# Splitting the finished mixed rows of two output projections during the attention units ahead of them

## The chip, the cores and the metric

One core of one Trainium2 chip runs the whole program as a single launch. The metric is device time in microseconds, the median of several runs. The engines are TensorE (PE, matmuls; PEld is its loading of stationary weights), VectorE (DVE), ScalarE (ACT), GpSimd (POOL) and SyncE (SP), which here issues nearly all DMAs. Each works through its own queue in order and waits on semaphores.

## The reference

Four residual layers over 256 tokens of width 2048, batch 1, in float32. The first two matter here:

```python
def even_layer(h, w_in, ..., w_out):
    lru_x, lru_gate, q, k, v, swa_gate = split_cols(h @ w_in, EVEN_SPLITS)
    y_a = rg_lru(conv(lru_x), ...) * silu(lru_gate)                # 1024 columns
    y_b = sliding_window_gqa_sinks(q, k, v, sinks) * silu(swa_gate) # 1024 columns
    return jnp.concatenate([y_a, y_b], axis=-1) @ w_out            # 2048 x 2048

def odd_layer(h, w_in, ..., w_out):
    y_c = causal_mla_attention(q, k_c, v_c) * silu(mla_gate)       # 1024 columns
    y_d = rmsnorm(causal_diff_attention(qd, kd, vd, lam), subln) * silu(diff_gate)
    return jnp.concatenate([y_c, y_d], axis=-1) @ w_out            # 2048 x 2048

x = x + even_layer(rmsnorm(x, g0), ...)
x = x + odd_layer(rmsnorm(x, g1), ...)
```

A second block of two layers (retention and Fourier mixing, then a gated convolution) follows, with a context of 256 tokens and shifts, scales and gates that come from conditioning matrices `ada_w`.

## The kernel before

**Precision.** Each float32 operand is split in two: a high half rounded to TensorE's float32r type, and a low half, the difference. A product is three matmuls: high by high, high by low, low by high (L1742 to L1744 where weights are stationary, L1753 to L1755 where activations are). ScalarE writes the high half of weights (`w_hi`, L656), VectorE the low half (`w_lo`, L1159). The projected activations live as both halves in `act` (`act_hl`, 16 tiles of 128 features by 2 x 256 tokens), the split operand of the next projection.

**Stages, units, pieces.** The work is a row of stages: lru, kv, swa, out0, cq, diff, mla, out1, ret, four, out2, conv, out3. A stage is cut in units (an eighth or a quarter of its output columns), a unit in pieces of weights (swa, out0, mla and out1 have 4 units of 8 pieces). A piece is about 128 x 1024 numbers in one of 4 slots: SP loads it to `w_raw`, ScalarE and VectorE split it, TensorE multiplies. A slot is split again when TensorE has used the piece four back (`s_used`, "piece_used"), and loaded again when VectorE has split it (`s_lo`).

**Hooks.** All five engines run the same loop over pieces. After its own step for piece p, an engine calls a hook, `hook(p)`. In unit i + 1 the hook does the rest of unit i: for swa, the hooks compute scores (TensorE, hook 0, L1991), maxima (VectorE, hook 3, L1317 to L1329), exponentials (ScalarE, hook 4), normalised probabilities (VectorE, hook 4, up to L1343), transposes (TensorE, hook 4, L1998), values times probabilities (TensorE, hook 6, L2004 to L2006), and the gated result into `y` (`y_mix`, VectorE, hook 7, L1362). mla is alike, with rotated queries (L1420 to L1423) ahead of the scores and its result at L1432. The hooks of the last unit of swa run in unit 0 of out0, those of mla's last in unit 0 of out1. TensorE issues the last unit's scores before piece 0 of the output projection, and its transposes behind piece 2.

**Mixed rows.** The inputs of an output projection are the 16 tiles of `y`, split into `act` by `mix(stage, q)` in four groups of four tiles: ScalarE copies the high half (L662, from L717), VectorE subtracts (L1262). Group 0 is needed by piece 0 (`inputs_ready`), the next ones by pieces 2, 4 and 6. The order of the groups is

```python
        FOURS = [(4 * q, 4) for q in range(4)]
        GROUPS = {"out0": FOURS, "out1": [FOURS[0], FOURS[2], FOURS[3], FOURS[1]]}
```

so in out0 groups 0 and 1 are the lru rows, in out1 group 0 is the first half of mla, groups 1 and 2 are diff. The last group is the one that the last unit finishes. `act` is the operand of swa's own projections, and of the first four pieces of each mla unit; the other four read `cn` (`c_norm`), the normalised latents, 10 tiles that cq writes. In the kernel before, groups 0 to 2 are split in hook 2 of unit 0 of the output projection, when all pieces of the stage ahead are used.

**Beside it.** VectorE also multiplies and sums conditioning weights (`ada_step`, L1148) in hooks of swa, out0, cq, diff, mla and out1: behind pieces 0, 1, 5 and 6 in swa, behind every piece in mla and in units 1 to 3 of out0. The output projection of unit i is added to `x_res` in hook 2 of unit i + 1 (L1505).

Of the kernel before, what the change touches and what calls it, by code (L numbers as in the profile page):

```python
# [55 lines left out]
COUNT = {s: n for s, n, _ in STAGES}  # L56
# [93 lines left out]
def build(nc, d, out, stop_after=None):  # L150

    ctx = ExitStack()
    with ctx:
# [134 lines left out]
        S = {}  # L288
# [306 lines left out]
        def mix_dst(stage, kt):  # L595
            second = stage in ("out2", "out3") and not (isinstance(kt, int) and kt >= KT)
            return (act2, kt) if second else (act, kt % KT)
# [48 lines left out]
        def _(sc):  # L646
# [400 lines left out]
            if wanted("kv"):  # L1047
                split("kv")(0, lambda p: lru(p, COUNT["lru"] - 1))
                stage_loop(sc, "swa", split("swa"), swa, kv)
            if wanted("out0"):  # L1050
                n = COUNT["swa"] - 1
                post0, sums0 = out_sums("out0")
                stage_loop(sc, "out0", split("out0"), post0, placed({
                    2: [step(swa, 2, n), projections_through("out0"), *mixes("out0", 0, 1, 2), step(swa, 4, n)],
                    5: [step(swa, 6, n)],
                    6: [y_ready("swa"), *mixes("out0", 3)]}))
# [5 lines left out]
            if wanted("diff"):  # L1062
                stage_loop(sc, "diff", split("diff"), diff, cq_end)
                stage_loop(sc, "mla", split("mla"), mla, squeezed(diff, COUNT["diff"] - 1))
            if wanted("out1"):
                n = COUNT["mla"] - 1
                post1, sums1 = out_sums("out1")
                stage_loop(sc, "out1", split("out1"), post1, placed({
                    2: [step(mla, 2, n), projections_through("out1"), *mixes("out1", 0, 1, 2), step(mla, 4, n)],
                    5: [step(mla, 6, n)],  # L1070
                    6: [y_ready("mla"), *mixes("out1", 3)]}))
# [47 lines left out]
        def _(ve):  # L1119
# [546 lines left out]
            if wanted("kv"):  # L1666
                split("kv")(0, lambda p: lru(p, COUNT["lru"] - 1))
                stage_loop(ve, "swa", split("swa"), swa, kv)
            if wanted("out0"):
# [3 lines left out]
                    2: [*mixes("out0", 0), step(swa, 3, n), *mixes("out0", 1, 2), step(swa, 4, n)],  # L1673
# [5 lines left out]
            if wanted("diff"):  # L1679
# [6 lines left out]
                stage_loop(ve, "mla", split("mla"), mla, diff_end)  # L1686
            if wanted("out1"):
# [3 lines left out]
                    2: [step(mla, 3, n), *mixes("out1", 0, 1, 2), step(mla, 4, n)],  # L1691
# [567 lines left out]
```

How the kernel before makes its waits and increments, by code:

```python
            def load_ada(stage, i, a, k):  # L459
                if not isinstance(a, int) or a >= ADA_RING:
                    sp.wait_ge(s_au, a - (ADA_RING - 1))
                layer = 1 if stage in ("ret", "conv") else 0
                first = {"ret": i * ADA_N, "four": (i - 1) * ADA_N + 2 * D, "conv": (i - 1) * ADA_N + 2 * D}
                first = first[stage] if stage in first else a // ADA_K * ADA_N
                w = d["ada_w_2"].rearrange("l (t p) n -> p l t n", p=P)
                sp.dma_start(ada_ring_of(stage)[:, k % ADA_RING, :], w[:, layer, k, ds(first, ADA_N)])\
                    .then_inc(s_aw[k % ADA_RING], 16)
# [2 lines left out]
                def load(i, hook, first=0):  # L471
                    for p in range(PIECES[stage]):
                        g = PIECE0[stage] + PIECES[stage] * i + p
                        pieces = sources(stage, i, p)
                        if not isinstance(g, int) or g >= RING:
                            sp.wait_ge(s_lo, g - (RING - 1))
                        for dst, src in pieces:
                            sp.dma_start(dst(w_raw[:, p % RING, :]), src).then_inc(s_w[p % RING], 16)
                        for a, k in ada_steps(stage, first, i, p):
                            if stage == "ret" and first == 0 and k == 0:
                                sp.wait_ge(s_n["psum"], NORM_BANKS[3] + 8)
                            if stage == "four" and first == 1 and k == 0:
                                sp.wait_ge(S["ret"]["o"], COUNT["ret"])
```

## Time and profile before

| what | value |
|---|---|
| median of 3 runs | 2867.1 us (2862.36 to 2867.46) |
| the profiled execution | 2870.17 us, of which the span 2868.5 |
| TensorE busy | 2737.6 us (95% of the span), loads 2568.2 |
| VectorE busy | 1763.1 us (61%) |
| ScalarE busy | 1280.6 us (45%) |
| DMA | 534.50 MB, 186 GB/s on average |
| mean granted clock of TensorE | 0.978 |

The span runs from the first to the last instruction; the rest of the execution lies around it. Busy shares are averages over all stages. The granted clock is a share of TensorE's 2.4 GHz: 1.00, or 0.50 for 1.2 GHz.

### The profile page before, as it was taken

Reading aid. Unit: us, or ns where it says so; the run is one execution under the profiler, and the core shown is the slowest. Engines: PE = TensorE matmul, PEld = TensorE weight load, DVE = VectorE, ACT = ScalarE, POOL = GpSimd, SP = SyncE. Lnnn points to the kernel's source line nnn. Section 1 sums busy time; section 2 is a strip of 40 time slices with the busy share of each in tenths; the row PEclk is TensorE's granted clock in tenths of the full one; section 3 lists DMA queues with packets and bytes.
Section 4 is the critical chain, followed back from the end, with each engine's and each line's share of the span. In section 5 each row is a group of like instructions: output and inputs, shape, how many; then the busy total and the mean of one; then the engine's idle time right before and its main releaser. Section 6 shows DMA issues by size and latency. Waiting matters only on the chain.

```text
span 2868.5 us, 49783 instructions
## 1 busy us (share of the span) xinstructions
PE 2737.6 (95%) x19249; PEld 2568.2 (90%) x19249; DVE 1763.1 (61%) x2244; ACT 1280.6 (45%) x1670; POOL 18.4 (1%) x33
## 2 busy tenths in 40 slices
PE   7999999998889799999999999999999999999997
PEld 7998789998777699999999987879999999999786
DVE  6777878777656755555556535456675454555544
ACT  5556444554443434443343334444444444444443
POOL 1000000000000000000000000000000000000000
PEclk9999999998889899999999999999999999999999
DMA  6565866655537365555548644547685555555554
GB/s 185 151 196 159 271 185 204 186 178 173 162 129 271 104 197 167 176 177 185 174 156 277 207 147 154 188 144 250 228 292 180 186 182 181 181 180 185 175 189 139
DMA packets 450700, 534.50 MB, mean 186 GB/s; under 512 B 32955, under 2 KB 343750, under 8 KB 449670
## 3 DMA queue, kind: packets, MB, share of 16 engines
q1 hardware_dynamic: 447840, 522.29, 57.5%
q0 software_dynamic: 2064, 10.11, 1.1%
q8 instruction: 92, 1.51, 0.2%
q14 instruction: 42, 0.34, 0.0%
q10 hardware_dynamic: 662, 0.25, 0.0%
HBM read 530.46 MB, written 2.10 MB: 186 GB/s over the span
## 4 chain that ended last, share of the span: by engine, by line
PE 82%; DVE 7%; ACT 3%; DVEq 3%; DMA 2%; issue 2%; ACTq 0%; SPq 0%
PE banks L1742 16%; PE banks L1744 16%; PE banks L1743 16%; PE banks L1753 8%; PE banks L1754 8%; PE banks L1755 8%; DVE w_lo L1159 3%; ACT w_hi L656 2%; PE banks L1991 1%; PE banks L2120 1%; PE banks L2137 1%; PE banks L1899 1%; DVEq L1150 1%; DMA w_raw<-in_od_w_in 1%; DMA w_raw<-in_l_w_in 1%
## 5 line engine op out<-in xcount | busy, mean ns | idle before, releaser
L1159 DVE TENSOR_TENSOR w_lo<-w_raw,w_hi 128x1024 fp32r<-128x1024 f32 (+2 forms) x848 | 974.5, 1160 | 834.1 <-ACT w_hi L656 814.0
L656 ACT ACTIVATE w_hi<-w_raw 128x1024 fp32r<-128x1024 f32 (+2 forms) x848 | 844.4, 1005 | 1088.5 <-PE banks L1744 606.1
L1742 PE MATMUL banks<-act_hl,w_hi 128*128 128x256 f32 x4304 | 1249.1, 290 | 36.0 <-DVE w_lo L1159 17.1
L1744 PE MATMUL banks<-act_hl,w_lo 128*128 128x256 f32 x4304 | 1226.0, 285 | 0.0
L1743 PE MATMUL banks<-act_hl,w_hi 128*128 128x256 f32 x4304 | 1225.9, 285 | 0.0
L1742 PEld LDWEIGHTS banks<-act_hl,w_hi 128*128 128x128 f32 x4304 | 832.9, 194 | 52.3 <-DVE w_lo L1159 18.7
L1743 PEld LDWEIGHTS banks<-act_hl,w_hi 128*128 128x128 f32 x4304 | 832.9, 194 | 3.8 <-issue 2.4
L1744 PEld LDWEIGHTS banks<-act_hl,w_lo 128*128 128x128 f32 x4304 | 832.5, 193 | 0.0
L1753 PE MATMUL banks<-w_hi,act_hl 128*128 128x512 f32 (+3 forms) x1440 | 509.5, 354 | 26.4 <-DVE x_res L1505 7.5
L1754 PE MATMUL banks<-w_lo,act_hl 128*128 128x512 f32 (+3 forms) x1440 | 506.9, 352 | 0.0
L1755 PE MATMUL banks<-w_hi,act_hl 128*128 128x512 f32 (+3 forms) x1440 | 506.2, 352 | 0.0
L1753 PEld LDWEIGHTS banks<-w_hi,act_hl 128*128 128x128 f32 x1440 | 273.8, 190 | 66.4 <-DVE w_lo L1159 13.5
L1755 PEld LDWEIGHTS banks<-w_hi,act_hl 128*128 128x128 f32 x1440 | 273.3, 190 | 32.6
L1754 PEld LDWEIGHTS banks<-w_lo,act_hl 128*128 128x128 f32 x1440 | 273.6, 190 | 31.4 <-issue 0.2
L662 ACT ACTIVATE scr_b<-banks 128x512 f32<-128x512 f32 (+3 forms) x130 | 77.5, 619 | 112.6 <-PE banks L2137 29.8
L1148 DVE SCALAR_TENSOR_TENSOR acc_x<-const_b,silu_c,acc_x 128x512 f32<-128x512 f32 x120 | 89.8, 748 | 4.5
L1148 DVE SCALAR_TENSOR_TENSOR acc_x<-y_mix,silu_c,acc_x 128x512 f32<-128x512 f32 x120 | 89.5, 746 | 1.7
L1148 DVE SCALAR_TENSOR_TENSOR acc_c<-ada_ring,silu_c,acc_c 128x512 f32<-128x512 f32 x120 | 89.4, 745 | 0.1
L1148 DVE SCALAR_TENSOR_TENSOR acc_x<-ada_ring,silu_c,acc_x 128x512 f32<-128x512 f32 x120 | 89.4, 745 | 0.0
L662 ACT ACTIVATE scr_a<-banks 128x512 f32<-128x512 f32 (+2 forms) x68 | 42.4, 662 | 92.4 <-PE banks L1998 55.4
L777 ACT ACTIVATE scr_a<-scr_a,soft 128x128 f32<-128x128 f32 x80 | 35.3, 442 | 52.7 <-DVE soft L1329 52.7
L1932 PE MATMUL banks<-ident,x_res 128*128 128x128 f32 x128 | 21.2, 332 | 20.6 <-DMA x_res<-in_x 10.8
(270 smaller groups left out, 1586.5 us busy)
## 6 DMA issues: line engine op xcount, KB each, us to landing
w_raw<-in_od_w_in SPq DMA_DIRECT2D x256, 512.0 KB, 4.5
w_raw<-in_ev_w_in SPq DMA_DIRECT2D x256, 256.0 KB, 3.6
w_raw<-in_l_w_in SPq DMA_DIRECT2D x96, 512.0 KB, 4.3
w_raw<-in_l_w_in SPq DMA_DIRECT2D x128, 256.0 KB, 3.2
ada_ring<-in_ada_w SPq DMA_DIRECT2D x128, 256.0 KB, 4.3
w_raw<-in_l_w_out SPq DMA_DIRECT2D x64, 512.0 KB, 4.9
y_mix<-in_ada_w SPq DMA_DIRECT2D x128, 256.0 KB, 3.1
const_b<-in_ada_w SPq DMA_DIRECT2D x128, 256.0 KB, 4.5
```

The source lines that it names most:

```text
L656: last = nc.scalar.activation(dst(w_hi[:, p % RING, :]), src(w_raw[:, p % RING, :]), ACT.Copy)
L662: return nc.scalar.activation(dst, src, ACT.Copy, **k)
L777: last = nc.scalar.activation(v[:, h, lo:hi], v[:, h, lo:hi], ACT.Exp, bias=soft[:, 1, 2 * h + b:2 * h + b + 1], accum_out=soft[:, 2, 2 * ...
L1148: last = stt(acc, w, cond, acc, ALU.mult, ALU.add)
L1150: drain()
L1159: last = tt(dst(w_lo[:, p % RING, :]), src(w_raw[:, p % RING, :]), dst(w_hi[:, p % RING, :]).bitcast(F32), ALU.subtract)
L1742: mm(out, hi, a[:, kt, 0:T], start=start, stop=False, skip_group_check=True)
L1743: mm(out, hi, a[:, kt, T:2 * T], start=False, stop=False, skip_group_check=True)
L1744: return mm(out, lo, a[:, kt, 0:T], start=False, stop=stop, skip_group_check=True)
L1753: mm(out, ah, hi, start=start, stop=False, skip_group_check=True)
L1754: mm(out, ah, lo, start=False, stop=False, skip_group_check=True)
L1755: return mm(out, al, hi, start=False, stop=stop, skip_group_check=True)
```

## The change

The whole splits of groups 0 and 1 move ahead. For out0 they go to unit 2 of swa (hooks 0 and 5 on ScalarE, 1 and 6 on VectorE) and write `cn`, which is not in use before cq; TensorE reads these eight tiles there. For out1 they go to unit 3 of mla (hooks 6 and 7 on both engines), when the unit's first four pieces have been used, and write `act` as before; group 2 goes to hook 0 of out1's unit 0. Group 3 stays. TensorE's order of instructions does not change, only an address.

```diff
         def mix_dst(stage, kt):
+            if stage == "out0" and kt < 8:
+                return cn, kt
             second = stage in ("out2", "out3") and not (isinstance(kt, int) and kt >= KT)
...
@@ ScalarE
-                stage_loop(sc, "swa", split("swa"), swa, kv)
+
+                def swa_and_mix(p, i):
+                    swa(p, i)
+                    if i == 1 and p in (0, 5):
+                        sc.wait_ge(S["lru"]["y"], COUNT["lru"] + 1)
+                        mix("out0", p // 5)
+                stage_loop(sc, "swa", split("swa"), swa_and_mix, kv)
...
-                    2: [step(swa, 2, n), projections_through("out0"), *mixes("out0", 0, 1, 2), step(swa, 4, n)],
+                    2: [step(swa, 2, n), projections_through("out0"), *mixes("out0", 2), step(swa, 4, n)],
...
-                stage_loop(sc, "mla", split("mla"), mla, squeezed(diff, COUNT["diff"] - 1))
+                def mla_and_mix(p, i):
+                    mla(p, i)
+                    if i == COUNT["mla"] - 2 and p in (6, 7):
+                        sc.wait_ge(s_used, pieces_before("mla", i + 1) + 4)
+                        mix("out1", p - 6)
+                stage_loop(sc, "mla", split("mla"), mla_and_mix, squeezed(diff, COUNT["diff"] - 1))
...
-                    2: [step(mla, 2, n), projections_through("out1"), *mixes("out1", 0, 1, 2), step(mla, 4, n)],
+                    0: mixes("out1", 2),
+                    2: [step(mla, 2, n), step(mla, 4, n)],
...
@@ VectorE
-                stage_loop(ve, "swa", split("swa"), swa, kv)
+                def swa_and_mix(p, i):
+                    swa(p, i)
+                    if i == 1 and p in (1, 6):
+                        mix("out0", p // 6)
+                stage_loop(ve, "swa", split("swa"), swa_and_mix, kv)
...
-                    2: [*mixes("out0", 0), step(swa, 3, n), *mixes("out0", 1, 2), step(swa, 4, n)],
+                    2: [step(swa, 3, n), *mixes("out0", 2), step(swa, 4, n)],
...
-                stage_loop(ve, "mla", split("mla"), mla, diff_end)
+                def mla_and_mix(p, i):
+                    if i == COUNT["mla"] - 2 and p in (6, 7):
+                        mix("out1", p - 6)
+                    mla(p, i)
+                stage_loop(ve, "mla", split("mla"), mla_and_mix, diff_end)
...
-                    2: [step(mla, 3, n), *mixes("out1", 0, 1, 2), step(mla, 4, n)],
+                    0: mixes("out1", 2),
+                    2: [step(mla, 3, n), step(mla, 4, n)],
```

How instructions move is shown on VectorE, at three places. The numbers of lines are 16 higher in the changed kernel, so L1159, L1262 and L1317 are L1175, L1278 and L1333 there.

In swa's unit 2, before, from the result of unit 0 (`y_mix`) to the start of unit 1's maxima (`soft` are the row statistics, `acc_c` and `acc_x` the conditioning sums):

```order
L1362 TENSOR_TENSOR y_mix<-banks,scr_a 128x512 [waits swa_gate,swa_o]
L1159 TENSOR_TENSOR w_lo<-w_raw,w_hi 128x1024 [waits piece_hi]
L1148 SCALAR_TENSOR_TENSOR acc_c<-ada_ring,silu_c,acc_c 128x512 [waits ada_landed0]
L1148 SCALAR_TENSOR_TENSOR acc_x<-ada_ring,silu_c,acc_x 128x512
L1159 TENSOR_TENSOR w_lo<-w_raw,w_hi 128x1024 [waits piece_hi]
L1148 SCALAR_TENSOR_TENSOR acc_c<-ada_ring,silu_c,acc_c 128x512 [waits ada_landed1]
L1148 SCALAR_TENSOR_TENSOR acc_x<-ada_ring,silu_c,acc_x 128x512
L1159 TENSOR_TENSOR w_lo<-w_raw,w_hi 128x1024 [waits piece_hi] x2
L1317 TENSOR_TENSOR scr_a<-banks,const_a 128x768 [waits swa_scores]
```

and in the changed kernel:

```order
L1378 TENSOR_TENSOR y_mix<-banks,scr_a 128x512 [waits swa_gate,swa_o]
L1175 TENSOR_TENSOR w_lo<-w_raw,w_hi 128x1024 [waits piece_hi]
L1164 SCALAR_TENSOR_TENSOR acc_c<-ada_ring,silu_c,acc_c 128x512 [waits ada_landed0]
L1164 SCALAR_TENSOR_TENSOR acc_x<-ada_ring,silu_c,acc_x 128x512
L1175 TENSOR_TENSOR w_lo<-w_raw,w_hi 128x1024 [waits piece_hi]
L1278 TENSOR_TENSOR c_norm<-y_mix,c_norm 128x4x256 [waits mix_hi]
L1164 SCALAR_TENSOR_TENSOR acc_c<-ada_ring,silu_c,acc_c 128x512 [waits ada_landed1]
L1164 SCALAR_TENSOR_TENSOR acc_x<-ada_ring,silu_c,acc_x 128x512
L1175 TENSOR_TENSOR w_lo<-w_raw,w_hi 128x1024 [waits piece_hi] x2
L1333 TENSOR_TENSOR scr_a<-banks,const_a 128x768 [waits swa_scores]
```

The subtraction of group 0 (`c_norm`) stands behind the `w_lo` of piece 1, ahead of that piece's conditioning sums; that of group 1 stands likewise behind piece 6, further down.

At out0's start, before, from the `w_lo` of the first three pieces, through the maxima of the last swa unit:

```order
L1159 TENSOR_TENSOR w_lo<-w_raw,w_hi 128x1024 [waits piece_hi] x3
L1262 TENSOR_TENSOR act_hl<-y_mix,act_hl 128x4x256 [waits mix_hi]
L1317 TENSOR_TENSOR scr_a<-banks,const_a 128x768 [waits swa_scores]
L1322 TENSOR_REDUCE soft<-scr_a 128x2
L1323 TENSOR_REDUCE soft<-scr_a 128x2
L1326 TENSOR_TENSOR soft<-soft,sinks 128x4
...
L1329 TENSOR_SCALAR soft<-soft 128x4
L1262 TENSOR_TENSOR act_hl<-y_mix,act_hl 128x4x256 [waits mix_hi] x2
L1355 TENSOR_TENSOR soft<-soft 128x4 [waits swa_exp]
```

and in the changed kernel:

```order
L1175 TENSOR_TENSOR w_lo<-w_raw,w_hi 128x1024 [waits piece_hi] x3
L1333 TENSOR_TENSOR scr_a<-banks,const_a 128x768 [waits swa_scores]
L1338 TENSOR_REDUCE soft<-scr_a 128x2
L1339 TENSOR_REDUCE soft<-scr_a 128x2
L1342 TENSOR_TENSOR soft<-soft,sinks 128x4
...
L1345 TENSOR_SCALAR soft<-soft 128x4
L1278 TENSOR_TENSOR act_hl<-y_mix,act_hl 128x4x256 [waits mix_hi]
L1371 TENSOR_TENSOR soft<-soft 128x4 [waits swa_exp]
```

The subtraction of group 0 ahead of the first maxima is gone, and of the two behind the second maxima one is left, that of group 2.

At out1's start, before, from the `w_lo` of the first three pieces (L1420 to L1423 are the rotated queries, then come the maxima of the last mla unit):

```order
L1159 TENSOR_TENSOR w_lo<-w_raw,w_hi 128x1024 [waits piece_hi] x3
L1420 TENSOR_TENSOR scr_a<-banks,const_a 128x256 [waits mla_rot]
L1421 TENSOR_TENSOR scr_a<-scr_a,const_a 128x256
L1423 TENSOR_TENSOR scr_a<-scr_a 128x256
L1317 TENSOR_TENSOR scr_a<-banks,const_a 128x768 [waits mla_scores]
L1322 TENSOR_REDUCE soft<-scr_a 128x2
L1323 TENSOR_REDUCE soft<-scr_a 128x2
L1329 TENSOR_SCALAR soft<-soft 128x4
L1262 TENSOR_TENSOR act_hl<-y_mix,act_hl 128x4x256 [waits mix_hi] x3
L1337 RECIPROCAL soft<-soft 128x4 [waits mla_exp]
```

and in the changed kernel:

```order
L1175 TENSOR_TENSOR w_lo<-w_raw,w_hi 128x1024 [waits piece_hi]
L1278 TENSOR_TENSOR act_hl<-y_mix,act_hl 128x4x256 [waits mix_hi]
L1175 TENSOR_TENSOR w_lo<-w_raw,w_hi 128x1024 [waits piece_hi] x2
L1436 TENSOR_TENSOR scr_a<-banks,const_a 128x256 [waits mla_rot]
L1437 TENSOR_TENSOR scr_a<-scr_a,const_a 128x256
L1439 TENSOR_TENSOR scr_a<-scr_a 128x256
L1333 TENSOR_TENSOR scr_a<-banks,const_a 128x768 [waits mla_scores]
L1338 TENSOR_REDUCE soft<-scr_a 128x2
L1339 TENSOR_REDUCE soft<-scr_a 128x2
L1345 TENSOR_SCALAR soft<-soft 128x4
L1353 RECIPROCAL soft<-soft 128x4 [waits mla_exp]
L1358 TENSOR_TENSOR scr_a<-scr_a,soft 128x2x128
```

The subtraction of group 2 stands between the first `w_lo` and the other two, ahead of the rotated queries; the three behind the maxima are gone.

## Rows read from the trace of the kernel before

**Rows 1.** The page: its span, and the chain that ended last (shares of the span).

```profile
span 2868.5 us, 49783 instructions
...
PE 82%; DVE 7%; ACT 3%; DVEq 3%; DMA 2%; issue 2%; ACTq 0%; SPq 0%
```

**Rows 2.** TensorE's timeline at out0's start: start us, duration us, then line and operation.

```profile
267.66 1.68 PE L1991 MATMUL banks<-scr_a 64*128 64x128 f32 x16
272.61 0.79 PE L1753 MATMUL banks<-w_hi,act_hl 128*128 128x512 f32 x1 [3.27 <-DVE act_hl L1262]
...
275.67 0.39 PE L1754 MATMUL banks<-w_lo,act_hl 128*128 128x512 f32 x1
...
282.02 0.39 PE L1755 MATMUL banks<-w_hi,act_hl 128*128 128x512 f32 x1
```

**Rows 3.** VectorE's timeline, same stretch.

```profile
265.31 3.49 DVE L1159 TENSOR_TENSOR w_lo<-w_raw,w_hi 128x1024 fp32r<-128x1024 f32 x3
...
272.48 0.95 DVE L1317 TENSOR_TENSOR scr_a<-banks,const_a 128x768 f32<-128x768 f32 x1
...
277.47 2.35 DVE L1262 TENSOR_TENSOR act_hl<-y_mix,act_hl 128x1024 fp32r<-128x1024 f32 x2
...
281.99 0.68 DVE L1343 TENSOR_TENSOR scr_a<-scr_a,soft 128x512 f32<-128x512 f32 x1
```

**Rows 4.** ScalarE's timeline, same stretch.

```profile
270.26 2.93 ACT L662 ACTIVATE act_hl<-y_mix 128x1024 fp32r<-128x1024 f32 x3
273.21 1.28 ACT L772 ACT_TABLE_LOAD   x1
...
277.59 0.20 ACT L772 ACTIVATE soft<-soft 128x4 f32<-128x4 f32 x1 [0.53 <-DVE soft L1329]
...
279.46 2.94 ACT L656 ACTIVATE w_hi<-w_raw 128x1024 fp32r<-128x1024 f32 x3
```

**Rows 5.** Windows: us, busy of PE, PEld, DVE, ACT, POOL, then granted clock, DMA.

```profile
240.00:244.00 4.00, 4.00 (x38) 3.58 (x36) 3.91 (x5) 3.92 (x5) 0.00 (x0) 1.00 0.77 243
272.00:276.00 4.00, 3.39 (x9) 2.73 (x10) 3.70 (x9) 3.38 (x8) 0.00 (x0) 0.57 0.17 65
738.00:742.00 4.00, 4.00 (x31) 4.00 (x29) 3.76 (x8) 3.20 (x10) 0.00 (x0) 0.78 0.18 48
816.00:820.00 4.00, 4.00 (x28) 4.00 (x28) 3.84 (x8) 3.52 (x9) 0.00 (x0) 0.72 0.34 96
```

**Rows 6.** TensorE's timeline at out1's start.

```profile
840.90 0.46 PE L1991 MATMUL banks<-scr_a 128*128 128x128 f32 x2 [2.04 <-DVE scr_a L1423]
...
846.19 1.22 PE L1991 MATMUL banks<-k_rope,scr_a 64*128 64x256 f32 x2
850.92 0.80 PE L1753 MATMUL banks<-w_hi,act_hl 128*128 128x512 f32 x1 [3.51 <-DVE act_hl L1262]
...
855.78 0.42 PE L1755 MATMUL banks<-w_hi,act_hl 128*128 128x512 f32 x1
```

**Rows 7.** VectorE's timeline, same stretch.

```profile
836.10 3.50 DVE L1159 TENSOR_TENSOR w_lo<-w_raw,w_hi 128x1024 fp32r<-128x1024 f32 x3
...
849.64 3.49 DVE L1262 TENSOR_TENSOR act_hl<-y_mix,act_hl 128x1024 fp32r<-128x1024 f32 x3
```

**Rows 8.** Timeline of swa unit 2, VectorE and TensorE.

```profile
225.51 0.68 DVE L1343 TENSOR_TENSOR scr_a<-scr_a,soft 128x512 f32<-128x512 f32 x1
...
227.65 1.47 PE L1998 MATMUL banks<-ident,scr_a 128*128 128x128 f32 x12
...
236.64 0.69 DVE L1362 TENSOR_TENSOR y_mix<-banks,scr_a 128x512 f32<-128x512 f32 x1 [3.83 <-PE banks L2006]
```

**Rows 9.** TensorE's timeline: scores of mla units 1 and 3, pieces behind them.

```profile
729.20 0.46 PE L1991 MATMUL banks<-scr_a 128*128 128x128 f32 x2 [2.22 <-DVE scr_a L1423]
...
736.37 0.58 PE L1742 MATMUL banks<-act_hl,w_hi 128*128 128x256 f32 x1
...
813.02 0.58 PE L1742 MATMUL banks<-act_hl,w_hi 128*128 128x256 f32 x1
```

## The prediction

> **What bounds the kernel now.** I read the page first: the chain that ended last is 82% TensorE [rows 1]. Only TensorE's idle time, and time it works at the lower clock, can be won. So I went through TensorE's timeline for idle stretches over 0.3 us around both projections, then looked at VectorE and ScalarE beside each, then at the granted clock.
>
> At out0, the last scores of swa end at 267.66 + 1.68 = 269.34, and the first out0 matmul starts at 272.61, after 3.27 us of waiting for VectorE's subtraction L1262, which writes the low half of the first mixed rows [rows 2]. What is late there is ScalarE: it runs the three copies of mixes 0, 1, 2 from 270.26, behind other work, and VectorE has been free since 268.80 [rows 3, 4]. The weights of pieces 0 to 2 were ready by then: those are the three w_lo that end at 268.80.
>
> The matmuls after that stretch also run slow: the granted clock in 272 to 276 is 0.57 [rows 5], a mixture of 1.2 and 2.4 GHz, and TensorE was idle for 3.27 us before it fell. From 275.67 on they run at full pace [rows 2].
>
> At out1, the wait is 3.51 us, from 846.19 + 1.22 = 847.41 to 850.92, for the same VectorE line [rows 6]: there VectorE waits for the scores themselves, computes the row maxima, and only then subtracts three groups [rows 7]. The clock is already at 1.2 GHz when the scores of this unit run, and stays so until 855.78, where the matmul takes 0.42 us and no longer 0.8 [rows 6].
>
> **The change, part by part.** *Out0, removed.* Groups 0 and 1 are split in swa unit 2, so pieces 0 to 3 need nothing from unit 3. TensorE can start piece 0 right behind its scores, at 269.35. Three pieces are 36 matmuls. From 275.67 to 282.02 there are 28 steps, so 0.227 us each at full clock: 36 take 8.2 us and end at 277.6. Before, they took 9.8 us (272.61 to 282.41), 1.6 of it through the clock. If the clock stays up I therefore gain 3.3 + 1.6 there.
>
> What is late next is the transposes behind piece 2: they wait for the probabilities, which ended at 281.99 + 0.68 = 282.67 [rows 3]. VectorE now starts the first maxima at 268.8 instead of 272.48, has one subtraction of 1.2 us between instead of two (2.27 us from 277.47 to 279.74, less one: 1.14 saved). From 272.48 to 282.67 are 10.19 us; less 1.14 they are 9.05, so 268.8 + 9.05 = 277.9. ScalarE must keep up: one copy from 270.26 ends at 271.3, its table load (1.28) at 272.6, each pair of exponentials takes 1.9 (277.59 to 279.46) [rows 4], so 274.5 and 276.4; VectorE reads the second at 276.5. That fits. The transposes start at 278.0 instead of 282.73: **4.7 us**. ScalarE's w_hi of pieces 3 to 5 then start at 276.4 instead of 279.46 [rows 4], in time. If the clock falls all the same, the pieces take 9.8 us from 269.35 and end at 279.2: 3.5 us. These are the two ends; I take 4.7, since the stretch that preceded the fall is gone and the same scores followed directly by pieces ran at full clock in unit 3 of swa (240 to 244, clock 1.00 [rows 5]).
>
> *Out0, added in swa unit 2.* Two copies on ScalarE of about 1.0 us (2.93 for three [rows 4]) and two subtractions of 1.2 on VectorE [rows 3]. ScalarE has idle time there. VectorE gets the first before its own maxima, so the probabilities of this unit end 1.14 later: 225.51 + 0.68 + 1.14 = 227.3, and TensorE asks for them at 227.65 [rows 8]. The cover is 0.3 us thin. The second comes behind piece 6, ahead of a stretch in which VectorE idles 3.83 us [rows 8]. Cost 0; if the cover is gone, 1 us at most, for it would be the whole subtraction. Queued behind them are the conditioning sums and, on SP's queue, the loads that wait for them; these have no stall of their own here.
>
> *Out1, removed and moved.* Groups 0 and 1 go to the last mla unit: ScalarE's copies behind the copy of the transposed probabilities, VectorE's subtractions ahead of the unit's last step. VectorE waits there for ScalarE and so passes w_hi and values later, but in this stretch of its timeline it stands idle twice, behind ScalarE's w_hi of piece 7 and then behind TensorE's values; its three w_lo from 836.10 are the next thing that matters [rows 7]. I cost this at 0, with 1 us as the bound, one subtraction that sticks out.
>
> Group 2 goes to hook 0 of out1, and VectorE's subtraction now stands between the w_lo of piece 0 and those of pieces 1 and 2. Behind these come the rotated queries (L1420 to L1423), for which TensorE waits 2.04 us before the scores at 840.90 [rows 6]. So this subtraction is on the path: 3.49 / 3 [rows 7], **+1.15 us**. Scores start at 842.05 and take 6.5 us as before (840.90 to 847.41), so they end at 848.6. Piece 0 then starts at once, instead of at 850.92: **2.35 us** gained, in place of the 3.51 that stood there. The bound: if all scores run at 1.2 GHz they take 7.17, as from 729.20 to 736.37 [rows 9], and the gain is 1.7.
>
> Transposes behind piece 2 wait for nothing: even with three subtractions VectorE is done with them at 853.13, and two halves of normalising took 2.9 us at out0 (from 279.8 to 282.67 [rows 3]), so 856.0; TensorE arrives at 848.6 + 8.2 = 856.8 at the earliest. The clock: in two mla units where pieces follow the scores without a stretch between, the low clock reaches some way into the pieces: 3.4 us in the one (from 736.37 [rows 9] to 739.8, since the window 738 to 742 has 0.78 [rows 5]) and 5.2 in the other (from 813.02 [rows 9] to 818.2, since the window 816 to 820 has 0.72 [rows 5]). In out1 it is 4.9 (850.92 to 855.78). I take no difference, with 1.6 us either way, the loss of the low stretch at out0.
>
> Group 3 stays where it was in both projections, and everything after hangs on TensorE's own values. The waits of the next units for the additions L1505 end a chain of VectorE's that starts at those values; they move earlier with it and are neither won nor lost.
>
> Sum: 4.7 + 2.35 + 0 = 7.05 us off. Against the profiled execution (span 2868.5 [rows 1], 2870.17 with what lies around it) that is 2861.4 and 2863.1. The three timed runs have a median of 2867.1, 3.1 below the profiled one; against it I predict 2860.0.
>
> **What the skill says of it.** All this counts on the clock being given back at out0 (the trace shows it low for one stretch [rows 2, 5]). The Trainium skill, "TensorE: Matmul & The Clock Gate", Part 1, says that the count of slow matmuls at a start is "run-variable": one kernel measured 6, 11 or 14. By it, the 1.6 us seen in one profile need not be there in the timed runs of before, and the sum would be 5.4. The trace agrees in so far as the low parts of the two mla units differ (3.4 and 5.2 us) under the same work. I carry this as rival B.
>
> **The rivals.** *A, the forecast:* both waits go, with the clock at out0: 5.7 to 8.7 us, 0.55. For it speaks that both waits name L1262 and nothing else waits inside them.
>
> *B: only the waits go.* The low clock at out0 is not in the timed runs of before, or falls in those of after, or out1's low part gets longer: 3.3 + 2.35 = 5.6 down to 3.5 + 0.2 = 3.7 (2.35 less 0.65 of slower scores less 1.6). Against: in the profile the fall follows a stretch that goes. 2861.5 to 2863.5, centre 2862.5; 0.30.
>
> *C: the change is eaten by new waits.* The thin cover in swa unit 2 fails (1 us), and mla's subtraction holds the values and so the rotated queries (1 us) besides the 1.15 counted. 7.05 - 2 = 5 us remain, 3.5 if the clock gives nothing: 2862 to 2864, 0.09.
>
> *D: slower.* Mechanism: the low stretches after out1. Everything behind out0 shifts by about 5 and 7 us against whatever decides the clock; the waits of the later stages, as those before the scores of mla [rows 9], can then each draw a longer low stretch. One more of them costs 1.6 us, so it turns the sign from five of them on, net (5 x 1.6 = 8 against 7), and shows as slower by 0.2% from eight. For it: low stretches of very different length stand in the trace. Against: they can as well get shorter, and the same holds for any two runs of one kernel, whose three times lie 5.1 us apart. 2868 to 2873, 0.06.
>
> **How the numbers follow.** Faster by over 0.2% (5.7 us, about what a measurement of this kernel can tell from no change): A and a little of B, 0.57. Within: most of B and C, 0.38. Slower: 0.05. The range: from A's upper gain with 2.5 us of scatter between runs, 2867.1 - 8.7 - 2.5 = 2856, to rival C's, 2867.1 - 2, rounded to 2865.5; D lies outside. A's own range is 2858.4 to 2861.4.
>
> **What would show it.** Right: no idle TensorE between the scores and piece 0 of out0, clock 1.00 there, transposes less than 0.5 us after piece 2; at out1 the wait ahead of the scores grows from 2.04 to 3.2 and that behind them is gone; L1998 of swa unit 2 without a wait. Wrong: a wait of TensorE for L1343 in swa unit 2 or for a w_lo in the last mla unit, the values' multiplication L1432 later than TensorE's L2006 in that unit, or low stretches elsewhere that sum to more than the 3.4 us dropped.

## The result and the profile after

The changed kernel takes 2849.2 us (median of 10 runs, 2845.6 to 2860.0), the one before 2866.8 us on the same chip (median of 10, 2862.4 to 2869.0): a ratio of 0.9946, 95% interval 0.9934 to 0.9959. That is faster by more than measurement error, and by more than I had said: 17.6 us where I predicted 7.1, and 6.8 us below the lower end of the range.

The page of the changed kernel gives the span and TensorE's busy time. All its TensorE lines have moved by 28 (L1753 is now L1781, L1991 the scores L2019), VectorE's by 16, ScalarE's by 2.

```profile
span 2846.1 us, 49783 instructions
...
PE 2726.1 (96%) x19249; PEld 2559.3 (90%) x19249; DVE 1763.5 (62%) x2244; ACT 1280.2 (45%) x1670; POOL 18.3 (1%) x33
...
PE 82%; DVE 7%; ACT 4%; DVEq 3%; DMA 2%; issue 2%; ACTq 0%; SPq 0%
```

The same row of the kernel before, with the same count of instructions:

```profile
PE 2737.6 (95%) x19249; PEld 2568.2 (90%) x19249; DVE 1763.1 (61%) x2244; ACT 1280.6 (45%) x1670; POOL 18.4 (1%) x33
```

The chain is nearly what it was [rows 1]. The span is 22.4 us shorter, in two halves: TensorE idles 120.0 us instead of 130.9 (span less busy), and is busy 11.5 us less **with the same instructions**. That points to the clock. So there are two questions: did the waits go as predicted, and where did the clock come from?

**Out0.** TensorE's timeline at its start, to be laid beside [rows 2]:

```profile
267.31 1.68 PE L2019 MATMUL banks<-scr_a 64*128 64x128 f32 x16
268.93 0.50 PE L1781 MATMUL banks<-w_hi,c_norm 128*128 128x512 f32 x1
269.26 0.39 PE L1782 MATMUL banks<-w_lo,c_norm 128*128 128x512 f32 x1
269.49 0.39 PE L1783 MATMUL banks<-w_hi,c_norm 128*128 128x512 f32 x1
...
277.18 0.39 PE L1783 MATMUL banks<-w_hi,c_norm 128*128 128x512 f32 x1
277.69 1.53 PE L2026 MATMUL banks<-ident,scr_a 128*128 128x128 f32 x12
```

No idle time stands between scores and piece 0, all steps of the 36 matmuls but the first are short, and the transposes start at 277.69, 0.3 us before my 278.0. VectorE in the same stretch shows why: one subtraction now lies between the maxima and the probabilities, which end at 276.95 + 0.68 = 277.63 (282.67 in [rows 3]):

```profile
268.36 0.95 DVE L1333 TENSOR_TENSOR scr_a<-banks,const_a 128x768 f32<-128x768 f32 x1
...
273.37 1.22 DVE L1278 TENSOR_TENSOR act_hl<-y_mix,act_hl 128x1024 fp32r<-128x1024 f32 x1
...
276.95 0.68 DVE L1359 TENSOR_TENSOR scr_a<-scr_a,soft 128x512 f32<-128x512 f32 x1
```

**Out1.** TensorE's timeline, to be laid beside [rows 6]:

```profile
823.96 0.77 PE L2019 MATMUL banks<-scr_a 128*128 128x128 f32 x2 [3.18 <-DVE scr_a L1439]
...
830.28 1.22 PE L2019 MATMUL banks<-k_rope,scr_a 64*128 64x256 f32 x2
831.43 0.79 PE L1781 MATMUL banks<-w_hi,act_hl 128*128 128x512 f32 x1
...
833.73 0.53 PE L1783 MATMUL banks<-w_hi,act_hl 128*128 128x512 f32 x1
834.09 0.39 PE L1781 MATMUL banks<-w_hi,act_hl 128*128 128x512 f32 x1
```

The wait ahead of the scores grew from 2.04 to 3.18 us, as predicted for group 2's subtraction; the one behind them is gone. All scores ran at 1.2 GHz here (7.47 us, where my bound was 7.17), and the clock came back 2.6 us into the pieces, where it had been 4.9.

**Where the rest came from.** Four waits that stand in both kernels divide the span. TensorE's timeline of the kernel before:

```profile
304.22 0.47 PE L1753 MATMUL banks<-w_hi,act_hl 128*128 128x512 f32 x1 [2.11 <-DVE x_res L1505]
...
699.92 1.33 PE L1998 MATMUL banks<-ident,scr_a 128*128 128x128 f32 x5 [6.54 <-DVE scr_a L1403]
...
838.16 0.70 PE L2074 MATMUL banks<-scr_a,const_a 128*128 128x256 f32 x2 [1.02 <-ACT scr_a L662]
...
880.55 0.47 PE L1753 MATMUL banks<-w_hi,act_hl 128*128 128x512 f32 x1 [2.49 <-DVE x_res L1505]
```

and of the kernel after:

```profile
299.23 0.47 PE L1781 MATMUL banks<-w_hi,c_norm 128*128 128x512 f32 x1 [2.12 <-DVE x_res L1521]
...
692.90 0.90 PE L2026 MATMUL banks<-ident,scr_a 128*128 128x128 f32 x3 [6.54 <-DVE scr_a L1419]
...
820.08 0.70 PE L2102 MATMUL banks<-scr_a,const_a 128*128 128x256 f32 x2 [1.02 <-ACT scr_a L664]
...
859.95 0.47 PE L1781 MATMUL banks<-w_hi,act_hl 128*128 128x512 f32 x1 [2.49 <-DVE x_res L1521]
```

| stretch | before | after | gain |
|---|---|---|---|
| start to out0's second unit | 304.2 | 299.2 | 5.0 |
| out0's other units, cq and diff, to diff's last transposes | 395.7 | 393.7 | 2.0 |
| **mla, to its last rotation** | **138.2** | **127.2** | **11.1** |
| out1, to its second unit | 42.4 | 39.9 | 2.5 |
| the rest of the span | 1988.0 | 1986.1 | 1.8 |

Rows one and four are my two terms, 4.7 and 2.35. The biggest gain stands in mla, where the change costs little and saves nothing: of its 11.1 us, 9.5 are busy time (126.6 us before, 117.1 after), at a mean granted clock of 0.87 before and 0.94 after. Windows of both kernels at the scores of mla's units show what it is (columns as in [rows 5]). Before, units 1 to 3:

```profile
729.00:733.00 4.00, 3.80 (x10) 2.18 (x10) 0.06 (x1) 0.00 (x0) 0.00 (x0) 0.57 0.66 216
770.00:774.00 4.00, 4.00 (x10) 2.19 (x10) 0.00 (x0) 0.00 (x0) 0.00 (x0) 0.56 0.40 151
808.00:812.00 4.00, 4.00 (x10) 2.13 (x9) 0.00 (x0) 0.00 (x0) 0.00 (x0) 0.50 0.23 85
```

After:

```profile
721.50:725.50 4.00, 3.83 (x15) 2.37 (x16) 0.03 (x1) 0.00 (x0) 0.00 (x0) 1.00 0.62 232
757.00:761.00 4.00, 3.98 (x13) 2.54 (x14) 0.00 (x0) 0.00 (x0) 0.00 (x0) 0.74 0.67 233
793.00:797.00 4.00, 3.91 (x16) 2.37 (x16) 0.00 (x0) 0.00 (x0) 0.00 (x0) 1.00 0.66 211
```

Before, each unit ran its scores at 1.2 GHz and then some way into its pieces: a low stretch of 10.2 us, three times. After, these are 3.4 (at 714.5, ahead of the scores), 6.8 and none. The low stretches of the whole span sum to 128 us before and 101 after. TensorE was busy in 96 and in 72 us of them; 24 us at half the clock are worth 12, close to the 11.5 us of busy time that went. The wait alone does not decide it. Ahead of the scores of unit 3 it is the same in both kernels, and only the first has a low stretch there:

```profile
806.68 0.46 PE L1991 MATMUL banks<-scr_a 128*128 128x128 f32 x2 [1.63 <-DVE scr_a L1423]
```

```profile
793.09 0.46 PE L2019 MATMUL banks<-scr_a 128*128 128x128 f32 x2 [1.64 <-DVE scr_a L1439]
```

In the changed kernel's unit 2 the clock fell in the middle of the scores, under back-to-back work:

```profile
757.02 0.46 PE L2019 MATMUL banks<-scr_a 128*128 128x128 f32 x2 [2.16 <-DVE scr_a L1439]
...
757.83 0.70 PE L2019 MATMUL banks<-scr_a 128*128 128x256 f32 x2
758.46 0.80 PE L2019 MATMUL banks<-k_rope,scr_a 64*128 64x256 f32 x2
759.19 0.79 PE L2019 MATMUL banks<-scr_a 128*128 128x128 f32 x2
```

So the clock can also fall under work, some 2 us behind the end of the wait. The ten times of the changed kernel show that executions of one program differ: seven lie from 2845.6 to 2850.4, three at 2854.6, 2858.5 and 2860.0, while the ten of before lie within 6.6 us.

### The profile page after: what moved, and what is told of

The parts are those of the page before. It is cut to its first block, busy times and chain, and to the rows that moved or that the text cites. A ratio compares the mean times of both kernels' runs of the same rounds, so it can differ in the third digit from the quotient of the medians.

```text
span 2846.1 us, 49783 instructions
## 1 busy us (share of the span) xinstructions
PE 2726.1 (96%) x19249; PEld 2559.3 (90%) x19249; DVE 1763.5 (62%) x2244; ACT 1280.2 (45%) x1670; POOL 18.3 (1%) x33
## 4 chain that ended last, share of the span: by engine, by line
PE 82%; DVE 7%; ACT 4%; DVEq 3%; DMA 2%; issue 2%; ACTq 0%; SPq 0%
PE banks L1770 16%; PE banks L1772 16%; PE banks L1771 16%; PE banks L1781 9%; PE banks L1782 9%; PE banks L1783 9%; DVE w_lo L1175 3%; ACT w_hi L658 2%; PE banks L2019 1%; PE banks L2148 1%; PE banks L2165 1%; PE banks L1927 1%; DMA w_raw<-in_l_w_in 1%; DVEq L1166 1%; DMA w_raw<-in_od_w_in 1%
## 5 line engine op out<-in xcount | busy, mean ns | idle before, releaser
L1175 DVE TENSOR_TENSOR w_lo<-w_raw,w_hi 128x1024 fp32r<-128x1024 f32 (+2 forms) x848 | 974.7, 1160 | 822.5 <-ACT w_hi L658 802.7
L1781 PE MATMUL banks<-w_hi,act_hl 128*128 128x512 f32 (+3 forms) x1376 | 483.9, 352 | 15.1 <-DVE scr_b L1526 4.2
L1782 PE MATMUL banks<-w_lo,act_hl 128*128 128x512 f32 (+3 forms) x1376 | 481.8, 350 | 0.0
L1783 PE MATMUL banks<-w_hi,act_hl 128*128 128x512 f32 (+3 forms) x1376 | 481.5, 350 | 0.0
L1781 PEld LDWEIGHTS banks<-w_hi,act_hl 128*128 128x128 f32 x1376 | 261.8, 190 | 51.1 <-DVE w_lo L1175 8.3
L1783 PEld LDWEIGHTS banks<-w_hi,act_hl 128*128 128x128 f32 x1376 | 261.3, 190 | 29.9
L1782 PEld LDWEIGHTS banks<-w_lo,act_hl 128*128 128x128 f32 x1376 | 261.7, 190 | 29.1 <-issue 0.2
```

What stands on the lines that cost most here:

```text
L1175: last = tt(dst(w_lo[:, p % RING, :]), src(w_raw[:, p % RING, :]), dst(w_hi[:, p % RING, :]).bitcast(F32), ALU.subtract)
L1781: mm(out, ah, hi, start=start, stop=False, skip_group_check=True)
L1782: mm(out, ah, lo, start=False, stop=False, skip_group_check=True)
L1783: return mm(out, al, hi, start=False, stop=stop, skip_group_check=True)
```

## The experiments

**Theory P** (position): every unit of mla has a wait of 0.7 to 3.2 us ahead of its scores. Whether the clock falls there depends, by this theory, on where the wait and the scores stand against instants at which the chip sets the clock, and the kernel doesn't set those. Before, mla stood badly in nearly every execution; 5 us less upstream moved it. **Rival M**: something in the change makes mla itself faster. **Rival L**: luck of the profiled execution. E1 and e2 make one half of the change each.

E1 keeps out0's half; for out1, in both engines' programs:

```
-                    0: mixes("out1", 2),
-                    2: [step(mla, 3, n), step(mla, 4, n)],
+                    2: [step(mla, 3, n), *mixes("out1", 0, 1, 2), step(mla, 4, n)],
```

> 

> Only the out0 part of the change; out1 as in the kernel before. Theory P (phase): the instants at which the granted clock changes stand on a fixed beat within an execution, and taking 4.7 us out ahead of mla moves mla's scores against it; then most of the extra gain comes with this half alone: 4.7 local plus some 8 to 10 in mla, 2852 to 2855, and fewer low stretches at the scores of mla. Rival L (luck): the extra 10 us are drawn anew in each execution and belong to neither half; 4.7 less than before, 2862, with low stretches in mla as before. Rival M (mla): moving the splits into mla's last unit makes mla faster; then this half gives 4.7 alone, 2862.

E2 keeps out1's half; for out0:

```
-            if stage == "out0" and kt < 8:
-                return cn, kt
...
-                    2: [step(swa, 3, n), *mixes("out0", 2), step(swa, 4, n)],
+                    2: [*mixes("out0", 0), step(swa, 3, n), *mixes("out0", 1, 2), step(swa, 4, n)],
```

> 

> Only the out1 part; swa and out0 as in the kernel before. Theory P: nothing moves ahead of mla's scores, so mla's low stretches stay as before and only the local 2.35 (0.7 to 4) are won: 2864.4. Rival L: the same 2864, with more scatter. Rival M: the 10 us of mla come with this half: 2854.

E3 adds work to the kernel **before** and leaves out nothing: nine matmuls, 2.04 us, whose result nobody reads, in cq's second unit, ahead of its fifth piece. E4 does the same to the changed kernel with six (1.36 us).

```
+                        if stage == "cq" and first == 1 and p == 4:
+                            for _ in range(9):
+                                mm(bank(7), act[:, 0, 0:P], act[:, 0, :], start=True, stop=True,
+                                   skip_group_check=True)
```

> 

> The kernel before with nine more dense 128x512 matmuls (about 2.04 us of TensorE, into a bank that nobody reads) in unit 1 of cq, ahead of diff and mla. The work and the splits are otherwise those of before. Theory P: 2.0 us later stands against the clock's beat about where 4.7 us earlier does, so mla loses low stretches and the kernel is FASTER with work added: 2867 + 2.0 - 8, near 2861 (2857 to 2865). Rivals L and M: only the added work shows, 2869.

> 

> The changed kernel with six such matmuls (about 1.4 us) at the same place. Theory P: 4.7 - 1.4 = 3.3 us earlier than before is nearly where the kernel before stands against the beat, so mla's low stretches come back: 2849 + 1.4 + 8, near 2859 (2855 to 2862). Rivals L and M: only the added work, 2850.6.

| kernel | median, us | lowest to highest | ratio to before, 95% |
|---|---|---|---|
| e1, out0's half | 2859.9 | 2848.0 to 2861.6 | 0.9967 (0.9954 to 0.9981) |
| e2, out1's half | 2865.0 | 2859.6 to 2867.4 | 0.9997 (0.9988 to 1.0005) |
| e3, before + 2.04 us | 2855.1 | 2853.9 to 2859.9 | 0.9965 (0.9952 to 0.9978) |
| e4, changed + 1.36 us | 2859.2 | 2847.9 to 2863.3 | 0.9965 (0.9953 to 0.9977) |

The kernel before stood at 2866.8 us (25 runs) here. The halves give 6.9 and 1.8 us, 8.7 together, not 17.6 (for e2 the interval includes no gain at all); e1 has two runs at 2848.0 and 2850.3 and five at 2859.2 to 2861.6.

E1 is a miss for theory P, which said 2852 to 2855 us and fewer low stretches; its median lies nearer to the 2862 us of L and M, and its profile, one of the slower group, has all three:

```profile
729.00:733.00 4.00, 4.00 (x11) 2.46 (x11) 0.85 (x1) 0.00 (x0) 0.00 (x0) 0.50 0.00 0
766.00:770.00 4.00, 4.00 (x10) 2.03 (x9) 0.00 (x0) 0.00 (x0) 0.00 (x0) 0.50 0.20 75
804.00:808.00 4.00, 4.00 (x9) 2.25 (x10) 0.00 (x0) 0.00 (x0) 0.00 (x0) 0.50 0.15 57
```

Yet up to the last two pieces of mla e1 is the same program as the changed kernel, whose profile had one low stretch at the scores of units 1 to 3. So the upstream shift does not fix what an execution draws; at most it sets how often it draws the long stretches.

E3 is the plainest: **2 us more work and 11.7 us less time**, more even than P's 2857 to 2865. E4 gave back 10 us for 1.4 us of work, as P said (2855 to 2862), in two groups again: four runs at 2847.9 to 2850.8, eight at 2856.5 to 2863.3. Windows of e3 at its scores, units 1 to 3:

```profile
729.00:733.00 4.00, 3.32 (x15) 2.07 (x14) 0.56 (x2) 0.00 (x0) 0.00 (x0) 1.00 0.78 268
767.00:771.00 4.00, 4.00 (x10) 2.00 (x8) 0.00 (x0) 0.00 (x0) 0.00 (x0) 0.50 0.14 52
801.00:805.00 4.00, 3.75 (x15) 2.30 (x16) 0.11 (x1) 0.00 (x0) 0.00 (x0) 1.00 0.66 236
```

and of e4, whose profile is one of the slower group:

```profile
724.00:728.00 4.00, 4.00 (x10) 2.12 (x9) 0.00 (x0) 0.00 (x0) 0.00 (x0) 0.50 0.52 174
765.00:769.00 4.00, 4.00 (x9) 2.00 (x8) 0.00 (x0) 0.00 (x0) 0.00 (x0) 0.50 0.23 87
802.00:806.00 4.00, 4.00 (x9) 2.25 (x10) 0.00 (x0) 0.00 (x0) 0.00 (x0) 0.50 0.38 134
```

M falls: the kernel before gets the gain in mla without the change, and the changed kernel loses it without losing the change. L falls as the whole account, since the 25 runs of before (2863.6 us or more) and the five of e3 (2859.9 or less) do not overlap; what is left of it is that each execution of one kernel draws anew. What stays possible is that the added matmuls act on something else. So the next kernels take the position out of it: they fill the waits, so that TensorE is busy in them wherever they stand. E5 does this to the changed kernel, e6 to the kernel before.

```
                     te.wait_ge(s_free, bank_count("mla", i, 4))
+                    for _ in range(14):
+                        mm(half(7, 0), cn[:, 0, 0:P], cn[:, 0, 0:T], start=True, stop=True, skip_group_check=True)
                     te.wait_ge(s["rope"], i + 1)
```

> 

> The changed kernel with fourteen more matmuls of 128x256 c_norm columns (about 1.6 us at full clock, into an unused bank) in every unit of mla, placed in TensorE's wait for the rotated queries, which is 1.6 to 3.2 us long; their results are read by nobody. Theory P (the low stretches at mla's scores are ordered by how the idle wait stands to the clock's beat): with the wait filled no low stretch stands at any of mla's scores in any execution, so the slower of the two groups of times goes away: 2842 to 2848 us, all runs within 3 us of each other. Rival S (the scores' own 32-bit matmuls, not the wait, bring the clock down): low stretches stay where they are, 2849 to 2852 us with the same two groups. Rival W (the filling only delays the scores): 2850 to 2856 us.

> 

> The kernel before with the same fourteen matmuls in each of mla's waits for the rotated queries. Theory P: the four low stretches of 10.24 us at mla's scores go, which cost this kernel some 15 us against an execution without them: 2846 to 2854 us, though nothing of the change is in it. Rival S: 2866 to 2869 us, low stretches as before. Rival W: 2868 to 2872 us.

E7 puts group 2 of out1 back behind the third piece; e8 is e4 with three matmuls.

```
-                    0: mixes("out1", 2),
-                    2: [step(mla, 3, n), step(mla, 4, n)],
+                    2: [step(mla, 3, n), *mixes("out1", 2), step(mla, 4, n)],
```

> 

> The changed kernel with out1's group 2 back in the hook behind the third piece. By the prediction's sum the wait ahead of the last unit's scores is 2.04 us again in place of 3.18 us, but group 2's parts are late by about 1.2 us in the wait behind the scores: the time is the same within 1.5 us of the changed kernel's, 2848 to 2851 us. Theory P adds only that everything up to out1 keeps its two groups of times, since nothing ahead of it is moved. Rival M (that the placing of group 2 is what won time in mla): 2855 us or more.

> 

> The changed kernel with three more matmuls of 128x512 (0.68 us) in the second unit of cq. Theory P: a shift that lies between the changed kernel's and that of the six-matmul kernel; the two groups of times (about 2849 and about 2859 us) stay, and the share of the slower one lies between 3 in 10 and 8 in 12; median anywhere from 2849 to 2859 us. A theory in which added work costs its own length: 2849.9 us, one group.

| kernel | median, us | lowest to highest | ratio to before, 95% |
|---|---|---|---|
| e5, changed, filled | 2838.6 | 2834.8 to 2842.8 | 0.9910 (0.9893 to 0.9928) |
| e6, before, filled | 2850.1 | 2847.1 to 2850.4 | 0.9943 (0.9928 to 0.9957) |
| e7, group 2 back | 2849.4 | 2843.2 to 2856.9 | 0.9949 (0.9932 to 0.9966) |
| e8, changed + 0.68 us | 2852.1 | 2847.5 to 2854.1 | 0.9951 (0.9935 to 0.9967) |

The kernel before: 2865.6 us (11 runs). The idle time is needed to bring the clock down here, and filling it is enough to keep the clock up at the scores: e6, with nothing of the change, is as fast as the changed kernel. Its windows at the scores of units 1 to 3 and of out1:

```profile
730.00:734.00 4.00, 3.77 (x15) 2.29 (x16) 0.18 (x1) 0.00 (x0) 0.00 (x0) 1.00 0.62 215
765.00:769.00 4.00, 3.57 (x16) 2.07 (x14) 0.42 (x1) 0.00 (x0) 0.00 (x0) 1.00 0.72 248
799.00:803.00 4.00, 4.00 (x17) 2.31 (x17) 0.14 (x1) 0.00 (x0) 0.00 (x0) 1.00 0.45 154
828.00:832.00 4.00, 4.00 (x20) 2.52 (x19) 0.18 (x1) 3.97 (x6) 0.00 (x0) 1.00 0.68 254
836.00:840.00 4.00, 4.00 (x10) 3.19 (x11) 3.93 (x6) 1.66 (x5) 0.00 (x0) 0.51 0.00 0
```

The last row is the stretch behind out1's wait of 3.51 us, which the fill does not touch and the change takes away. Before, the low stretch at out1 was 13.7 us long, not the 10.24 of my forecast for e6, and 6.8 of it stay. E5 beat its forecast by 3.4 us, and its runs lie 8 us apart where I expected 3, so mla was not the only place. E7 says that the place of group 2 is a matter of less than the scatter, and has P's two groups, three runs at 2843.2 to 2846.0 and three at 2852.9 to 2856.9. E8's median lies between those of the changed kernel and e4, as a shift's might, but without the two groups I had expected.

The next four join the two kinds: e9 is e5 with e4's six matmuls, e10 is e6 with e3's nine. E11 is e5 with the wait for the probabilities in diff filled as well, and e12 the kernel before with six added matmuls. The edit of e11:

```
                 if p == 7:
+                    te.wait_ge(s["max"], i + 1)
+                    for _ in range(40 if isinstance(i, int) and i == COUNT["diff"] - 1 else 18):
+                        mm(half(7, 0), cn[:, 0, 0:P], cn[:, 0, 0:T], start=True, stop=True, skip_group_check=True)
                     te.wait_ge(s["prob"], i + 1)
```

> 

> The changed kernel with mla's waits filled and with the six extra matmuls of 128x512 (1.36 us) in cq, which cost the unfilled one 10.0 us (2849.2 to 2859.2 us). Theory P (those 10 us were low stretches at mla's scores that the shift drew in): with the waits filled the same shift costs only its own length, 2838.6 + 1.4 = 2840.0 us, within 2 us. Rival C (the six matmuls cost 10 us by something else, in cq, diff or behind mla): 2847 us or more.

> 

> The kernel before with mla's waits filled and with nine extra matmuls (2.04 us) in cq, which made the unfilled one 11.7 us faster (2866.8 to 2855.1 us). Theory P (the gain was low stretches in mla that the shift dodged): they are gone already, so the nine matmuls now cost their length, 2850.1 + 2.0 = 2852.1 us, within 2 us. Rival C (nine matmuls in cq gain by themselves): 2840 us or less.

> 

> The changed kernel with mla's waits filled and, too, the wait for the weights in each unit of diff (18 matmuls of 128x256, some 2.0 us of 2.87; 40 in the last unit, some 4.5 us of 6.5). Theory P: the low stretches of 3.4 us at 530 and 588 us and that of 6.8 us at 690 us go; full clock in them gives back at most half of 13.6 us and less where the engine waits anyway: 2832 to 2836 us. Rival S (only mla's scores answer to filling): 2838 to 2840 us, with the stretches where they are.

> 

> The kernel before with six extra matmuls (1.36 us) in cq: a point between before (2866.8 us) and its nine-matmul form (2855.1 us). A cost that goes by the number of matmuls gives 2859 us. Theory P gives two levels instead, set by which of mla's four units still draw 10 us of low clock: near 2867 us or near 2856 us, or both among the runs, with a span of 5 us or more between them.

| kernel | median, us | lowest to highest | ratio to before, 95% |
|---|---|---|---|
| e9, e5 + 1.36 us | 2839.0 | 2836.3 to 2843.8 | 0.9906 (0.9891 to 0.9922) |
| e10, e6 + 2.04 us | 2851.6 | 2851.3 to 2851.8 | 0.9945 (0.9932 to 0.9959) |
| e11, e5 + diff filled | 2836.1 | 2835.5 to 2837.2 | 0.9893 (0.9877 to 0.9908) |
| e12, before + 1.36 us | 2857.9 | 2854.1 to 2867.8 | 0.9966 (0.9954 to 0.9978) |

The kernel before: 2867.3 us (10 runs). The shift that cost 10.0 us costs 0.4 once the waits are filled (four runs each, some 8 us apart), and the one that gained 11.7 us now costs 1.5 (five runs each, 3.3 and 0.5 us apart). So rival C falls: what the added matmuls gain or cost goes through the idle waits of mla. That the chip's own instants decide which waits are hit fits all of this, but no run sets them, so this part of P is argued and not shown. E12 has one run at 2867.8 and five at 2854.1 to 2860.3, which is P's "both among the runs", though its median alone would fit a cost by the number of matmuls (2859). E11 is the fastest of all, 1.1% below the kernel before; its 2.5 us below e5 lie within the scatter of e5's four runs. Windows of the changed kernel in diff (the last row holds the end of its last unit):

```profile
530.00:534.00 4.00, 3.99 (x21) 4.00 (x22) 3.91 (x5) 1.75 (x2) 0.00 (x0) 0.57 0.40 110
588.00:592.00 4.00, 4.00 (x21) 4.00 (x22) 3.91 (x5) 1.76 (x2) 0.00 (x0) 0.57 0.42 113
691.00:697.00 6.00, 4.10 (x19) 4.11 (x20) 5.74 (x8) 1.95 (x3) 0.00 (x0) 0.50 0.45 127
```

and of e11:

```profile
530.00:534.00 4.00, 3.28 (x29) 3.08 (x28) 3.93 (x5) 1.28 (x2) 0.00 (x0) 1.00 0.41 127
588.00:592.00 4.00, 3.75 (x32) 3.75 (x33) 3.91 (x6) 1.76 (x2) 0.00 (x0) 1.00 0.36 90
...
691.00:697.00 6.00, 5.36 (x46) 5.36 (x47) 5.82 (x9) 2.23 (x4) 0.00 (x0) 1.00 0.40 114
```

One thing was left. With mla filled in both, the change is still worth 11.5 us (e6 less e5), and my two terms make 7.1. The last three kernels have e11's two fills on the kernel before (e13), on out0's half alone (e14, otherwise e1) and on out1's (e15, otherwise e2).

> 

> The kernel before with the waits of mla and of diff filled: the base for the two kernels beside it. Theory P: below the form with only mla filled (2850.1 us) by what the low stretches at 380, 536, 594, 648 and 696 us cost, 2 to 6 us: 2844 to 2848 us. If the 11.5 us between the two mla-filled kernels are what the change is worth in itself, this kernel stands at 2847.6 us (2836.1 + 11.5); if part of it was clock in diff, at 2843 to 2846 us (2836.1 + 7 to 10).

> 

> Only the change's part at out0, with the waits of mla and diff filled. The prediction's term for out0 is 4.7 us; with the clock of everything behind it held up, the part should now be worth just that: 4 to 6 us below the kernel beside it without the part. Rival D2 (out0 is worth more by itself, since something else in diff waits less): 7 us or more.

> 

> Only the change's part at out1, with the waits of mla and diff filled. The prediction's term is 2.35 us, made of 3.51 us won and 1.15 us lost in the wait for the rotated queries; the wait that was won is also what brings the clock down for 6.8 us behind it (833 to 840 us), so 2.4 us by the waits alone and up to 3.4 us more by the clock: 2.4 to 5.8 us below the kernel beside it without the part. Rival N (out1 is worth nothing, as it looked in the run of this half alone, 0.9997): within 1 us.

| kernel | median, us | lowest to highest | below e13 | term predicted |
|---|---|---|---|---|
| e13, no part of the change | 2844.5 | 2840.9 to 2846.5 | | |
| e14, out0's half | 2838.9 | 2835.9 to 2841.5 | 5.6 | 4.7 |
| e15, out1's half | 2841.7 | 2840.3 to 2843.3 | 2.8 | 2.35 |
| e11, both (measured earlier, with e9) | 2836.1 | 2835.5 to 2837.2 | 8.4 | 7.05 |

With the clock held up, the halves add up to the whole, and the whole is 8.4 us: each term within 1 us, about the scatter of such a median. Out0's half is clear of it; out1's is barely so, and rival N's 1 us is not excluded by e13 and e15 alone, though e14 less e11 gives 2.8 us for it again. E13 lies 5.6 us below e6, so diff's waits cost clock as well, and the other 3.1 of the 11.5 us went when they were filled. Against the kernel before (2867.0 us) the ratios are 0.9924, 0.9906 and 0.9917, each within 0.0014.

## Why the prediction was wrong

**The two waits: right, in mechanism and size.** Out0's wait is gone, its clock is 1.00 and the transposes came at 277.69 for my 278.0; the stretch gained 5.0 us in the profile (0.35 of it was there before out0 begins) and 5.6 in e14, for 4.7. Out1 gained 2.5 us in the profile and 2.8 in e15, for 2.35, with the 1.15 us in front of the scores just as worked out. Two of its parts missed and in part cancelled, which is luck: the scores took 7.5 us and not 6.5, and the low stretch ended 2.3 us earlier in the pieces. I had misread [rows 6]: the first scores there ran at full clock (0.46 us at 840.90, for 0.77 in the changed kernel; the granted clock was 1.00 from 838.0 to 842.1), so it was not yet at 1.2 GHz when they began. One cost had no term: the matmuls on `c_norm` step 6 ns wider, some 1.2 us over the 192 of out0 by my estimate.

**The local zeros: right.** L1998 of swa unit 2 (now L2026, at 227.30) had no wait, and nothing in the last mla unit waited for a w_lo. E7 bears out that group 2's place is nearly neutral.

**The step that failed** is the last zero of the sum. The text costs the waits behind out0 by the work in them ("they move earlier with it and are neither won nor lost") and the clock by "no difference, with 1.6 us either way". What was mis-sized is the clock of everything that is moved, put at zero. It is 10.5 us of the 17.6 by difference, and filling the waits takes back 9.2 of it (6.1 in mla, from 17.6 to 11.5, and 3.1 in diff). It is not a scatter around zero either: in the profile of before, mla's units had all drawn 10.2 us of low clock, so a shift had little to lose there and much to win. I had the mechanism in hand as rival D ("can then each draw a longer low stretch"), gave it one sign, and set it aside with "they can as well get shorter", without reading from the windows how the stretches stood. Had I done so for units 1 to 3 of mla, I would have found all of them at their longest, and written a rival E: the shift dodges them, 3 x 10.2 us of low clock at half speed, up to 15 us. Its price was in the rows; its chance was not, since no view of the kernel before says where another position would stand.

**The price of D was too small too.** "One more of them costs 1.6 us" took the 3.4 us stretch of out0 for the unit of cost. A whole one in mla is worth some 4.5 us: the last unit of mla, with a low stretch of 10.2 us, took 39.4 us before (797.8 to 837.2), and without one 34.9 after (784.2 to 819.1).

**Rival B** read the remark of the Trainium skill as doubt about 1.6 us at out0. The Trainium skill, "TensorE: Matmul & The Clock Gate", Part 1, calls the cost of such starts under 1% of a span and run-variable. In these runs both hold (e4's two groups lie some 10 us, 0.35%, apart), yet 0.35% was more than the whole forecast. And it isn't random over kernels: in all its 67 timed runs the kernel before stood at 2857 to 2871 us, and two microseconds more work in cq brought it to 2853.9 to 2859.9.

**What stays open.** The 2.0 us up to diff's end are 0.5 us lost in out0's other units and 2.6 won at a low stretch of 6.8 us at 647.6 that the changed kernel's profile lacks; that it is the same cause I argue from e11 and e13. Of the 1.8 us behind out1, 1.4 lie at a low stretch near 1914 (10.2 us before, 6.8 after); 1.5 more come between 2009 and 2142, where the wait for `w_lo` is 1.1 us shorter, and 1.2 are lost ahead of both. None of this was tried. Why the kernel before stands badly nearly always, and the changed one, it seems, in 3 runs of 10, was not tried beyond the four shifts.

## What to carry to other kernels

When TensorE is the bound and short waits recur, a change upstream is worth its own time plus what the shift does to every recurring wait downstream, and the second can be larger. Before predicting, read the granted clock at each recurrence of a wait: if all are low the shift can mostly win, if none is it can mostly lose; one profile is one draw, as e1 shows. When measuring, run the kernel with a microsecond or two of unused matmuls added ahead, or with the waits filled; only a gain that survives both belongs to the change. And filling short waits of a repeated unit with matmuls nobody reads is itself a gain here: 15.5 us on the kernel before (e6), 10.6 on the changed one, for 14 matmuls a unit.

## What the hardware showed that I had not expected

- The clock fell behind waits of 1.6 to 3.2 us when they were followed by small 32-bit matmuls (128 columns), and did not when the waits were filled with 128x256 ones, although the same scores followed (e5, e6: clock 1.00 at all scores of mla). Nor did it fall each time: behind 1.63 us it was low for 10.2 us in the kernel before, behind 1.64 us not at all in the changed one.
- It could fall under back-to-back matmuls, not at the wait's end (between 758.46 and 759.19 in the changed kernel).
- More work made the kernel faster: 2.04 us of matmuls, 11.7 us less (e3).
- With c_norm as the operand the step of out0's pieces is 0.233 us (269.49 to 277.18, 33 steps), with the usual operand it was 0.227 (from 28 steps of [rows 2]), and so it is in the changed kernel's own pieces 4 to 7; 36 of the wider ones take 8.4 us where I had counted 8.2. Its cause was not tried.
